# The first norm's scale row, spread over the partitions by two matmuls instead of by a broadcast load

## The reference, cut to what matters

```
h   = x * rsqrt(mean(x*x) + 1e-6) * norm_mix_pre      # the norm that the change touches
p   = h @ w_in                                        # 1024 x 1792, split among three mixers
      pool mixer, gated convolution, sliding-window attention with sinks
x   = x + rms_norm(concat(mixers) @ w_o, norm_mix_post)
h   = rms_norm(x, norm_ffn_pre)
up  = causal_dwconv(h @ ffn_w_up) + ffn_conv_b
x   = x + rms_norm((silu(gate) * val) @ ffn_w_down, norm_ffn_post)
```

## Time and profile before

| What | Value |
|---|---|
| median of 3 runs | 950.43 us (950.13 to 950.52) |
| profiled execution, from its first instruction to its last | span of 948.2 us |
| median of the runs less the span | 2.2 us |
| PE busy | 938.9 us, 99% of the span |
| DVE busy | 654.7 us, 69% |
| ACT busy | 433.5 us, 46% |
| POOL busy | 189.4 us, 20% |

### The profile page before, as it was taken

One profiled execution on the slowest core, in us unless ns is written; L12 is line 12 of the kernel. 1 busy time (PEld: TensorE's weight loads), 2 busy tenths in 40 slices (PEclk: granted clock), 3 DMA queues, 4 the chain that ended last, 5 costly groups with the idle time before them and its releaser, 6 DMA issues.

```text
span 948.2 us, 11487 instructions
## 1 busy us (share of the span) xinstructions
PE 938.9 (99%) x4419; PEld 777.9 (82%) x4419; DVE 654.7 (69%) x710; ACT 433.5 (46%) x648; POOL 189.4 (20%) x182
## 2 busy tenths in 40 slices
PE   8999999999999999999999999999999999999997
PEld 7988887887888888888888888888888888888886
DVE  6645795766655899777877787778776653535668
ACT  5524444444433555445443444444444454335353
POOL 3301000000111424242223333443431100000021
PEclk9999999999999999999999999999999999999999
DMA  6999971005322236486343446554647775677455
GB/s 225 269 328 231 209 145 45 23 23 178 134 89 89 90 97 206 142 184 183 115 141 100 145 112 133 112 143 105 140 91 208 201 235 214 228 267 264 163 171 200
DMA packets 114248, 151.16 MB, mean 159 GB/s; under 512 B 6289, under 2 KB 66193, under 8 KB 114193
## 3 DMA queue, kind: packets, MB, share of 16 engines
q1 hardware_dynamic: 100737, 118.63, 38.5%
q0 software_dynamic: 13456, 31.79, 16.8%
HBM read 113.17 MB, written 60.29 MB: 183 GB/s over the span
## 4 chain that ended last, share of the span: by engine, by line
PE 97%; DVE 1%; DMA 0%; ACT 0%; POOL 0%; issue 0%; DVEq 0%; POOLq 0%; SPq 0%; ACTq 0%
PE ps L1616 30%; PE ps L1618 30%; PE ps L1617 30%; PE ps L1626 1%; PE ps L1751 1%; PE ps L1774 1%; PE ps L1752 1%; PE ps L1760 1%; PE ps L1778 1%; DMA xin<-in_x 0%; DVE hlo L1138 0%; PE ps L1789 0%; DVE ps L1155 0%; PE ps L1664 0%; DVE x2b L1427 0%
## 5 line engine op out<-in xcount | busy, mean ns | idle before, releaser
L1616 PE MATMUL ps<-hhi,whi 128*128 128x512 f32 (+1 forms) x240 | 91.1, 379 | 0.5 <-DVE hlo L1138 0.5
L1618 PE MATMUL ps<-hhi,wlo 128*128 128x512 f32 (+1 forms) x240 | 88.5, 369 | 0.0
L1617 PE MATMUL ps<-hlo,whi 128*128 128x512 f32 (+1 forms) x240 | 88.5, 369 | 0.0
L686 POOL TENSOR_TENSOR w_sums<-wraw 128x1024 f32<-128x1024 f32 x20 | 48.4, 2421 | 185.8 <-DVE w2lo L1373 63.0
L648 POOL TENSOR_SCALAR meansq<-sumsq 128x1 f32<-128x1 f32 x28 | 10.0, 357 | 373.4 <-ACT yg L1042 170.8
L1616 PEld LDWEIGHTS ps<-hhi,whi 128*128 128x128 f32 x240 | 45.3, 189 | 8.0 <-DVE hlo L1138 0.7
L1001 ACT ACTIVATE yg<-ps,par_b 128x1024 f32<-128x1024 f32 x21 | 25.3, 1207 | 57.9 <-DVE ps L1499 57.9
L1618 PEld LDWEIGHTS ps<-hhi,wlo 128*128 128x128 f32 x240 | 45.2, 189 | 7.7
L1617 PEld LDWEIGHTS ps<-hlo,whi 128*128 128x128 f32 x240 | 45.3, 189 | 7.4 <-issue 0.5
L1447 DVE SCALAR_TENSOR_TENSOR yg<-ps,par_a,yg 128x1023 f32<-128x1023 f32 x22 | 28.2, 1282 | 26.9 <-ACT yg L1001 26.9
L1616 PE MATMUL ps<-h2hi,whi 128*128 128x512 f32 x116 | 45.4, 391 | 0.2 <-DVE wraw L1148 0.2
(11 more groups left out here) (261 smaller groups left out, 2709.1 us busy)
## 6 DMA issues: line engine op xcount, KB each, us to landing
wraw<-in_ffn_w_up SPq DMA_DIRECT2D x42, 512.0 KB, 5.2
s_dram<-in_ffn_w_down POOLq DMA_DIRECT2D x6, 2816.0 KB, 28.1
wraw<-r_dram SPq DMA_DIRECT2D x44, 256.0 KB, 3.7
wraw<-s_dram SPq DMA_DIRECT2D x44, 256.0 KB, 4.9
r_dram<-cst SPq DMA_DIRECT2D x33, 256.0 KB, 2.8
wraw<-act_dram SPq DMA_DIRECT2D x33, 256.0 KB, 3.6
wraw<-in_ffn_w_down SPq DMA_DIRECT2D x33, 256.0 KB, 4.6
wraw<-in_w_in SPq DMA_DIRECT2D x14, 512.0 KB, 10.2
```

The source lines that it names most:

```text
L686: pool.tensor_tensor(w_sums[:, 0:2, :], raw[:, 0:4:3, :], raw[:, 2:3, :].broadcast_to([P, 2, HALF]), ALU.add)\
L1616: pe.matmul(acc, w_hi, x_hi, start=first, stop=False, skip_group_check=looped)
L1617: pe.matmul(acc, w_hi, x_lo, start=False, stop=False, skip_group_check=looped)
L1618: return pe.matmul(acc, w_lo, x_hi, start=False, stop=last, skip_group_check=looped)
```

## The change

The scale row is loaded once, as one row of 1024 in one partition (`gain_row`), from ACT's queue. A row of 128 ones times this row, as two matmuls of 512 columns, puts the same scales into all 128 partitions of PSUM banks 2 and 3. DVE copies both banks to `gain_a`. Every tile, the first two too, is then normed and scaled in `norm_x` in one instruction. The 512 KB broadcast load, the eight-row load, the small transpose and `scale_turned` are gone. The load of the identity matrix moves from SP's to ACT's queue. The eight `keep_clock` matmuls become three, the two with the ones, and three more.

```
--- before
+++ after
@@ SP
             load_x(0)
             load_x(1)
-            sp.dma_start(cst[:, 0:P], consts[:, 0:P]).then_inc(ident_in, 16)
-            sp.dma_start(gain_rows[0:KD, :], norm_mix_pre[0].rearrange("(k p) -> k p", p=P))\
-              .then_inc(gain_rows_in, 16)
             load_in(0)
             load_x(2)
             load_x(3)
-            sp.dma_start(gain_a[:, :], norm_mix_pre.broadcast_to([P, DM])).then_inc(gain_in, 16)
             load_in(1)
@@ POOL
+            pool.memset(ones[0:1, :], 1.0).then_inc(set_, 1)
             pool.memset(power[:, :], -0.5).then_inc(set_, 1)
@@ ACT
             def round_h(i, hi):
-                if i < 2:
-                    act.wait_ge(scaled, i + 1)
                 act.wait_ge(turned, i + 1)
...
+            act.dma_start(gain_row[0:1, :], norm_mix_pre[:, :]).then_inc(gain_row_in, 16)
+            act.dma_start(cst[:, 0:P], consts[:, 0:P]).then_inc(ident_in, 16)
             square_x(0)
@@ DVE
             def norm_x(t):
                 dve.wait_ge(rstd_ready, t + 1)
-                if t < 2:
-                    dve.tensor_scalar(hrow_a[:, t, :], xin[:, t, :], rstd[:, t:t + 1], None,
-                                      ALU.mult).then_inc(hrow_ready, 1)
-                    return
-                if t == 2:
-                    dve.wait_ge(gain_in, 16)
                 dve.scalar_tensor_tensor(hrow_a[:, t % 2, :], xin[:, t % 3, :], rstd[:, t:t + 1],
                                          gain_a[:, :], ALU.mult, ALU.mult)\
                    .then_inc(hrow_ready, 1)
...
+            for c in range(2):
+                cols = slice(c * HALF, (c + 1) * HALF)
+                dve.wait_ge(gain_spread, c + 1)
+                dve.tensor_copy(gain_a[:, cols], ps[:, 2 + c, :]).then_inc(gain_copied, 1)
+            dve.wait_ge(gain_copied, 2)
             norm_x(0)
             norm_x(1)
-            dve.wait_ge(gain_turned, 1)
-            finish_step(dve.tensor_copy(gain_t[:, :], ps[:, 3, 0:KD]))
-            scale_turned(0)
-            scale_turned(1)
             low_ring(0)
@@ PE
-            pe.wait_ge(set_, 3)
-            keep_clock(8)
+            pe.wait_ge(set_, 4)
+            keep_clock(3)
+            pe.wait_ge(gain_row_in, 16)
+            for c in range(2):
+                pe.matmul(ps[:, 2 + c, :], ones[0:1, :], gain_row[0:1, c * HALF:(c + 1) * HALF],
+                          start=True, stop=True).then_inc(gain_spread, 1)
+            keep_clock(3)
             pe.wait_ge(ident_in, 16)
-            pe.wait_ge(gain_rows_in, 16)
-            pe.transpose(ps[:, 3, 0:KD], gain_rows[0:KD, :], ident[0:KD, 0:KD]).then_inc(gain_turned, 1)
             turn_x(0)
             turn_x(1)
             keep_clock(4)
```

More of the change, by code:

```diff
@@ L159, in build @@
         hrow_a = alloc(xa, "hrow_a", [P, 2, DM])
-        gain_t = alloc(xa, "gain_t", [P, KD])
-        gain_rows = alloc(xa, "gain_rows", [P, P])
+        gain_row = alloc(xa, "gain_row", [P, DM])
+        ones = alloc(xa, "ones", [P, P])
         xa.close()
@@ L257, in build @@
         ident_in = sem("ident_in")
-        gain_rows_in = sem("gain_pre_in_as_eight_rows")
-        gain_turned = sem("gain_pre_on_channel_partitions")
-        scaled = sem("first_turned_rows_scaled")
+        gain_row_in = sem("gain_pre_in_as_one_row")
+        gain_spread = sem("gain_pre_over_partitions_in_psum")
         consts_in = sem("consts_in")
@@ L263, in build @@
         pool_w_in = sem("pool_w_in")
-        gain_in = sem("gain_pre_in")
+        gain_copied = sem("gain_pre_copied")
         gains_mix_in = sem("gains_mix_in")
@@ L655, in _ @@
                 root(i, i + 1)
-            pool.wait_ge(set_, 3)
+            pool.wait_ge(set_, 4)
             for g in range(4):
@@ L1198, in _ @@
                .then_inc(neg_ready, 1)
-            dve.wait_ge(set_, 3)
+            dve.wait_ge(set_, 4)
             dve.wait_ge(consts_in, 16)
@@ L1678, in keep_clock @@
                               start=True, stop=True)
-            pe.wait_ge(set_, 3)
-            keep_clock(8)
+            pe.wait_ge(set_, 4)
[5 more added lines that the diff above has]
+            keep_clock(3)
             pe.wait_ge(ident_in, 16)
-            pe.wait_ge(gain_rows_in, 16)
-            pe.transpose(ps[:, 3, 0:KD], gain_rows[0:KD, :], ident[0:KD, 0:KD])              .then_inc(gain_turned, 1)
             turn_x(0)
```

## The result

The changed kernel takes 952.63 us (median of 9 runs) against 950.15 (median of 9 runs of before): a ratio of 1.0022, with an interval from 1.0014 to 1.0030. It is 2.5 us slower. I had forecast 950.4 with a range to 952.0. What came is the third rival, in a milder form. Eight of the nine runs lie between 952.28 and 953.03, and one at 950.24, a spread that before doesn't have (950.08 to 950.52). This one run belongs to the explanation.

The account below looks back on a forecast made before the run. PE, at 97%, was taken to bound the kernel, the change moving only the dense part's start at 21.1 us. Span 948.2 + 2.2 + (0.0 ± 0.3) gave 950.4 us, range 949.6 to 952.0.

Parts of the forecast that it names:

- the third rival: PE at the start stays at the slow pace, through a stop or one-row weights: 954.4 us, chance 0.10.
- The row and PE's first work: Start of PE: row lands at 3.9, pace doubles at about 5 us, second ones matmul done at 6.3.
- the three unused matmuls behind the ones: PE ahead of the first turn: six records, 1.4 us, end at 7.7, costing nothing.
- The copies: DVE, PSUM to SBUF: 0.69 us for 512 columns, the second from 6.3 to 7.0.
- The hold on POOL: First norm holds POOL's root of tile 1, which ends at 8.75; second norm from 8.8 to 10.1.
- the second pair: Pair 1: norm of tile 2 catches POOL's first step for tile 3; root at 16.2, `norm_x(3)` at 16.2 as before.
- The first pass: PE, pair 0: starts at 12.3 against 12.24, behind ACT's rounding to 12.25.
- The third pass: PE, pair 0: directly follows the second pass, at 14.4 against 14.58, 0.2 us gained.
- The dense part: PE's back-to-back matmuls start at 21.1, as before.
- The row: Scale row's load on ACT's queue, issued at about 0.75, lands at 3.9; PE waits hardly at all.
- ACT's two issues: Two DMA issues ahead of ACT's first square, 0.84 us in idle time: nothing, or 0 to 0.3 us.
- nothing behind 21 us gives back or adds: Behind 21.1 us the same matmuls run back to back; the total moves only with the dense part's start.

Follow-up runs that it names:

- a_one_row_no_wait: Changed kernel, its one-row matmuls reading data from the tile of ones, PE waiting for the row only behind them and three unused matmuls: 952.33 us.
- b_one_row: Kernel before the change, the last five of its eight unused start matmuls using one row of weights and data instead of 128: 952.46 us, before 950.26.
- a_full_rows: Changed kernel, wait kept, the two matmuls with 128 rows of weights and data from the tile of ones instead of one: 950.33 us.
- a_interleaved: Changed kernel, same eight matmuls in another order: four unused, one one-row, one unused, one one-row, one unused: 955.00 us.
- c_by_halves: Complete version with zero-filled 128-row spreading and norms reading PSUM; DVE and POOL zero one half each, first norm waits per half: 949.54 us, before 950.26.
- a_half_rows: Changed kernel, the two matmuls with 64 rows from the tile of ones instead of one row: 950.51 us, in two groups.
- a_five_first: Changed kernel with five unused matmuls ahead of the one-row ones and one behind, instead of three and three: 953.51 us, ratio 1.0034.
- c_real_full: Changed kernel with zeroed row tile, 128-row spreading, norms of tiles 0 to 3 reading scales from PSUM, copies later, identity on SP: 950.21 us.

## Why the prediction was wrong, and where it was right

The failed step is in "The row and PE's first work": that the pace doubles at about 5 us as before, so that 2.7 of the four records of the ones take 1.3 us. They went on at 0.85 to 0.93 us each, and the second matmul was done at 8.0 instead of 6.3. I took the rise at 5 us from the earlier trace rows as a thing of time. In these kernels it hangs on what PE works on: with one-row matmuls in place of full ones it comes late, or early with a fall behind it (a_one_row_no_wait, b_one_row), and with full rows at the same place it comes early, by the times in all 11 runs (a_full_rows). The third rival named just this, "if matmuls with a single row of weights don't keep it up", but I gave it 0.10 together with the stop and priced it for a slow pace to 17 us. The pace doubled at some 12.4, so that it cost 2.4 us and not 4. (In a_interleaved, where the slow pace did last past 16 us, the time is 955.0, near the 954.4 of that rival.) The condition named there was right: the slow pace outlasted 8 us.

The sentence that the three unused matmuls behind the ones cost nothing fell with it. At the slow pace they ended at 10.9 in the chain, and the first turn, whose rows were ready at 10.1, waited behind them.

The rest of the working can be read in a_full_rows, where the clock rises in time. POOL and DVE in order of time:

```profile
6.34 0.69 DVE L1144 COPY gain_a<-ps 128x512 f32<-128x512 f32 x1 [0.17 <-PE ps L1668]
...
7.07 1.28 DVE L1121 SCALAR_TENSOR_TENSOR hrow_a<-xin,rstd,gain_a 128x1024 f32<-128x1024 f32 x1
7.24 1.16 POOL L644 TENSOR_SCALAR meansq<-sumsq 128x1 f32<-128x1 f32 x1 [0.65 <-ACT hrow_a L753]
...
8.48 0.55 POOL L647 TENSOR_TENSOR rstd<-meansq,power 128x1 f32<-128x1 f32 x1
...
9.07 1.29 DVE L1121 SCALAR_TENSOR_TENSOR hrow_a<-xin,rstd,gain_a 128x1024 f32<-128x1024 f32 x1 [0.72 <-POOL rstd L647]
```

- The copies: right. 0.69 us each, the second done at 7.03 (forecast 7.0), the first norm from 7.07 to 8.35 (7.05 to 8.33).
- The hold on POOL: right in kind; with it the second norm began 0.3 us later than forecast. It caught POOL's first step (1.16 us for 0.19) and not the second, because tile 1 had landed at 5.98. The second norm began at 9.07 instead of 8.8. The same hold came again in the second pair, as forecast (1.16 us at 14.73), and `norm_x(3)` began at 16.55 instead of 16.2. The lock between DVE with two SBUF inputs and GpSimd's reads, which the Trainium skill states ("SBUF — State Buffer", Who interferes with whom), thus shows in the trace: 1.16 us with both inputs in SBUF, and 0.19 and 0.56 us in c_by_halves, with one of them in PSUM.
- The first pass: 12.89 for 12.3. The hold made ACT's rounding of tile 1 end at 12.57; the rest is the four unused matmuls behind the second turn, which the sum had left out: the turn begins at 10.42, they follow at 11.35, and the pass, in line behind them, begins 2.47 us after the turn. From the forecast's own turn at 10.1 that gives 12.6, not 12.3. The third pass followed at 14.98 for 14.4. The dense part began at 21.42 for 21.1. The median, 950.33 for 950.4, is closer than the steps are; that much is luck.
- In the changed kernel itself the root of tile 1 was not held: the norms began at 8.80, when the roots of both tiles were done (8.31), so that the first norm waited for the ones alone. POOL's first step for tile 3 was held there too (1.16 us at 16.83).
- The row: it was there by 4.26, when PE began with the ones. That is no later than without the wait (a_one_row_no_wait), so that PE did not wait for it, and the forecast of 3.9 is not contradicted. It landed ahead of both tiles of x beside which it ran (4.73 and 6.2). ACT's two issues cost nothing: it was idle for 1.78 us ahead of its first square.
- That nothing behind 21 us gives back or adds: right. The start of the dense part moved by 2.39 us and the span by 2.5.

What stays open: why, with the same code, some executions of the changed kernel (1 of 9), of a_one_row_no_wait (3 of 11) and of a_half_rows (6 of 11) are as quick as before. None of their quick ones was profiled. In b_one_row none is quite as quick: its four lower runs lie 0.3 to 1.05 us above the median of before, all with a mean granted clock of 0.996 or 0.997 against 0.998 or 0.999 in the other seven, and in the one profiled the pace doubled, fell and rose again. What decides it stays unknown. Nor is it known why the pace doubled at about 5.0 us before and by 4.6 in the profiled run of b_one_row, whose first three matmuls are the same.

## What to carry to other kernels

A matmul with one row of weights takes as long as a full one (four records at the fast pace: 1.98 us in a_five_first, 1.95 with 128 rows in c_real_full), but in the first 8 us of this kernel it did not stand in for the full ones that brought the pace up. Ahead of moving PE work into a place where unused matmuls stood, compare what it is made of, not only how long it takes. The cure that worked here was to fill the other rows with zeros and keep all 128; zeroing the tile first let the row's load be issued only at 1.95 us (c_real_full) or 1.53 (c_by_halves) instead of 0.72. When times fall into two groups some 2 us apart, compare the pace of equal matmuls at the start of the trace.

A norm that read its scales from PSUM left POOL's steps at 0.19 and 0.56 us, and needed no copy ahead of it (c_real_full, c_by_halves). Where two engines hand a small result back and forth, look whether the larger instruction of the one holds the smaller one of the other, as the norm from SBUF did for 1.16 us.

## What the runs showed of the hardware that was not expected

- Two matmuls of 512 columns with one row in place of full ones cost 2.0 to 2.3 us of 952 (952.33 and 952.63 against 950.33), and 64 rows cost this in 5 of 11 runs.
- A clock that had risen fell again behind one-row work: it was 0.50 from 7.9 to 11.2 us in b_one_row and from 9.2 to 16.0 in a_five_first, the latter within an idle stretch. What it costs is how long PE is slow while it sets the pace of the others: 950.55 us for the first, 953.51 for the second, and 955.09 for a_interleaved, where the slow pace lasted past 16 us without a printed fall.
- At the start of a program the column of the granted clock shows 1.00 at either pace (0.42 and 0.21 us for equal records of 256 columns). It shows the falls that come later.
